# Inverting the diagonal blocks of a delta rule at 32x32 instead of 16x16, with a shorter plan of rounds

## The reference, cut to what matters

```
kb = kc * bc[..., None]
vb = vc * bc[..., None]
Lm = jnp.where(strict, jnp.einsum('nbhid,nbhjd->nbhij', kb, kc) * decay, 0.0)
A = Lm + jnp.eye(C)
rhs = jnp.concatenate([vb, kb * jnp.exp(gc)[..., None]], axis=-1)
sol = triangular_solve(A, rhs, left_side=True, lower=True, unit_diagonal=True)
uc, wc = sol[..., :DV], sol[..., DV:]
...
def step(S, xs):                      # scan over the chunks
    v_new = u_i - w_i @ S
    o = qg_i @ S + qk_i @ v_new
    S = S * gl_i + kg_i.T @ v_new
...
o = rms_norm(o, o_norm_w) * silu(z_b)
```

## Time and profile before

| | before |
|---|---|
| time, median of 3 runs (lowest to highest) | 1189.7 us (1189.56 to 1190.64) |
| the profiled execution's own time | 1193.43 us |
| its span (first to last instruction) | 1191.6 us |
| mean granted TensorE clock of the span | 0.981 |
| TensorE busy | 1154.5 us |
| VectorE busy | 611.9 us |
| ScalarE busy | 359.8 us |
| GpSimd busy | 218.9 us |

### The profile page before, as it was taken

One profiled execution on the slowest core, in us unless ns is written; L12 is line 12 of the kernel. 1 busy time (PEld: TensorE's weight loads), 2 busy tenths in 40 slices (PEclk: granted clock), 3 DMA queues, 4 the chain that ended last, 5 costly groups with the idle time before them and its releaser, 6 DMA issues. The chain is left out here.

```text
span 1191.6 us, 17445 instructions
## 1 busy us (share of the span) xinstructions
PE 1154.5 (97%) x6620; PEld 939.5 (79%) x6620; DVE 611.9 (51%) x1226; ACT 359.8 (30%) x706; POOL 218.9 (18%) x225
## 2 busy tenths in 40 slices
PE   7999999999999999999999999999999999999892
PEld 1588588888878888888788888888788898888671
DVE  2578645555257745563556644552555624445324
ACT  2356322246344211143344211233263301112001
POOL 1244324454200102310000103210000104221000
PEclk9999999999999999999999999999999979999897
DMA  9686754436765732226556621246734512123334
GB/s 369 193 338 226 249 207 158 160 134 223 281 215 209 220 111 90 88 107 239 198 207 211 191 106 72 107 142 230 279 140 146 160 44 100 71 71 107 135 114 166
DMA packets 78998, 203.03 MB, mean 170 GB/s; under 512 B 33674, under 2 KB 43658, under 8 KB 61380
## 3 DMA queue, kind: packets, MB, share of 16 engines
q1 hardware_dynamic: 78916, 201.91, 48.2%
HBM read 151.84 MB, written 50.05 MB: 169 GB/s over the span
## 5 line engine op out<-in xcount | busy, mean ns | idle before, releaser
L1936 PE MATMUL acc<-hhi,wsl 128*128 128x512 f32 x768 | 320.0, 417 | 0.0
L1938 PE MATMUL acc<-hhi,wsl 128*128 128x512 f32 x768 | 301.3, 392 | 0.0
L1937 PE MATMUL acc<-hlo,wsl 128*128 128x512 f32 x768 | 300.4, 391 | 0.0
L1938 PEld LDWEIGHTS acc<-hhi,wsl 128*128 128x128 f32 x768 | 144.6, 188 | 32.2
L1936 PEld LDWEIGHTS acc<-hhi,wsl 128*128 128x128 f32 x768 | 145.0, 189 | 31.4 <-issue 4.5
L1937 PEld LDWEIGHTS acc<-hlo,wsl 128*128 128x128 f32 x768 | 145.3, 189 | 26.5 <-issue 2.2
L1183 DVE SCALAR_TENSOR_TENSOR cacc<-raw,cw,cacc 128x512 f32<-128x512 f32 x144 | 112.8, 783 | 5.1
L1729 POOL TENSOR_TENSOR wsl<-wraw,wsl 128x512 fp32r<-128x512 f32 x64 | 86.2, 1364 | 129.8 <-ACT wsl L882 129.8
L911 ACT ACTIVATE raw<-acc 128x512 f32<-128x512 f32 x48 | 28.7, 597 | 187.3 <-PE acc L1938 179.7
L1180 DVE TENSOR_SCALAR cacc<-raw,cw 128x512 f32<-128x512 f32 x48 | 24.3, 506 | 91.2 <-ACT raw L911 89.7
L919 ACT ACTIVATE tmpa<-acc 128x512 f32<-128x512 f32 x32 | 19.0, 594 | 119.4 <-PE acc L1938 119.4
(11 more groups left out here) (289 smaller groups left out, 1974.4 us busy)
## 6 DMA issues: line engine op xcount, KB each, us to landing
wsl<-kept_w SPq DMA_DIRECT2D x96, 1024.0 KB, 4.8
kept_w<-wsl SPq DMA_DIRECT2D x32, 1024.0 KB, 6.3
wraw<-in_w SPq DMA_DIRECT2D x64, 256.0 KB, 4.2
wada<-in_w_ada SPq DMA_DIRECT2D x8, 1024.0 KB, 13.0
xb<-in_x SPq DMA_DIRECT2D x16, 512.0 KB, 5.5
xres<-in_x SPq DMA_DIRECT2D x16, 512.0 KB, 5.7
out_y<-ytok SPq DMA_DIRECT2D x16, 512.0 KB, 8.2
wada<-in_w_ada SPq DMA_DIRECT2D x16, 256.0 KB, 5.0
```

The costliest lines, as they stand in the source:

```text
L1936: nc.tensor.matmul(acc[t % 2][:], w[:, 0, k], hi[:, k], start=(k == 0), stop=False)
L1937: nc.tensor.matmul(acc[t % 2][:], w[:, 0, k], lo[:, k], start=False, stop=False)
L1938: last = nc.tensor.matmul(acc[t % 2][:], w[:, 1, k], hi[:, k], start=False, stop=(k == KT - 1))
```

## The change

The diagonal blocks that DVE inverts by substitution are 32x32 instead of 16x16. There are 64 of them, on 64 partitions (QB), and the steps are m = 1 to 30 instead of 1 to 14. LEVELS loses its 16. A round has five slots instead of seven, and there are 27 slots instead of 35.

- **Substitution.** It runs in three pieces: m = 1 to 10 after the convolution of tile 8, 11 to 19 after that of tile 9, 20 to 30 after that of tile 10. On DVE `zmul` of tile 12 stands ahead of the third piece, and `zmul` of tile 13 behind it; `zmul` of tile 14 moves to part 23. `inverses` moves from the load turn of tile 10 to that of tile 13, and writes two tiles, `xt` and `xn_`.
- **Plan.** HEAD is 32: four whole tiles (12 to 15) stand ahead of the first slot. FRONT becomes NC*NPREP-1. The last q = 3 falls on p = 6 of the closing slots. The samples' late steps go from slots 30 and 31 to 22 and 23.
- **ScalarE.** The silu of tile 11 moves from ahead of tile 12's tanh to behind that of tile 13.
- **Memory.** `xt` shares space with `ubuf`, `stmp` with `win`; the first u tile of a block waits for `yx`. The gate rows and their weights move to `htmp` and `gpw`, are loaded in block 0 once the samples' activations are turned (a new semaphore), and the row is stored two load turns later; `front_h` of the first block waits for that store.

```diff
-BS = 16
+BS = 32
-LEVELS = (16, 32, 64)
+LEVELS = (32, 64)
+QB = NBK * 16
-SLOTS = (NC + 1) * NPREP
+SLOTS = NC * NPREP + 7
-HEAD = 8
+HEAD = 32
-FRONT = NC * NPREP - 2
+FRONT = NC * NPREP - 1
-SUB_AT = 9
+SUB_AT = {8: (1, 11), 9: (11, 20), 10: (20, BS - 1)}
+INVERSES_AT = 13
...
-    return (r - 1, 3) if r == NC and p == NPREP - 1 else (None, None)
+    return (r - 1, 3) if r == NC and p == 6 else (None, None)
...
-        r, p = divmod(k, NPREP)
+        r, p = divmod(k, NPREP) if k < NC * NPREP else (NC, k - NC * NPREP)
...
-SAMPLE_SLOT = {... "joined": 30, "gate": 30, "pool": 30, "pooled": 31, "mixed": 31}
+SAMPLE_SLOT = {... "joined": 22, "gate": 22, "pool": 22, "pooled": 23, "mixed": 23}
...
+        ru = region("region_u", 4224)
+        ubuf = over("ubuf", ru, 0, [P, 2, BT + PB])
+        xt = over("xt", ru, 0, [QB, BS, BS])
+        rv_ = region("region_v", 4224)
+        win = over("win", rv_, 0, [P, 2, BT + PB])
+        stmp = over("stmp", rv_, 0, [QB, 256])
...
-        grow = ubuf[0:1 + NS].rearrange("p a b -> p (a b)")[:, 0:DM]
-        pwr = win[0:1 + NS].rearrange("p a b -> p (a b)")[:, 0:DM]
+        grow = htmp[0:1 + NS].rearrange("p a b -> p (a b)")
+        pwr = gpw[0:1 + NS]
...
SP, inverses():
-                sp.dma_start(xtd.rearrange("e q x -> q e x"), xtn[:].rearrange("p e j i -> p e (j i)")).then_inc(x_out, 16)
+                for e, blocks in enumerate((xt, xn_)):
+                    sp.dma_start(xtd[e], blocks[:].rearrange("p j i -> p (j i)")).then_inc(x_out, 16)
...
SP, block 0, t == 2:
+                            sp.wait_ge(*h_lo(PROLOGUE, 7))
+                            sp.wait_ge(*done("pe", "hs"))
+                            for dst, src in ((pwr, a["post_w"]), (grow, a["b_gate"])):
+                                sp.dma_start(dst[:], src.to_broadcast([1 + NS, DM])).then_inc(s_prm3, 16)
...
-                        if t == NQ + 6:
+                        if t == NQ + 8:
                             sp.wait_ge(s_trc, 4)
                             sp.dma_start(gate_rows, grow[1:1 + NS]).then_inc(gate_out, 16)
...
-                    if at == SUB_AT + 1:
+                    if at == INVERSES_AT:
                         inverses(it)
...
ACT, block_of():
-                silu_sq(it, NQ - 1)
...
+                        if n == 15:
+                            silu_sq(it, NQ - 1)
...
DVE, block_of():
-                    if t == SUB_AT:
-                        substitute(it)
+                    if t == 10:
+                        zmul(it, NQ)
+                    if t in SUB_AT:
+                        substitute(it, *SUB_AT[t])
+                    if t == 10:
+                        zmul(it, NQ + 1)
...
+                        if n == 23:
+                            zmul(it, t)
...
-                        if n < PARTS and n % 8 == 7 and tile_kind(t)[0] == "z":
+                        if n < PARTS and n % 8 == 7 and tile_kind(t)[0] == "z" and t >= NQ + 3:
                             gated(it, t)
```

More of the change, by code:

```diff
@@ L140, in pool_after @@
     return z - 4 if kind == "z" and z >= 4 else None
-SAMPLE_SLOT = {"spread": 0, "conv": 1, "square": 2, "sums": 4, "root": 5, "delta": 6, "rows": 8, "mean": 8, "joined": 30, "gate": 30, "pool": 30,
-               "pooled": 31, "mixed": 31}
+SAMPLE_SLOT = {"spread": 0, "conv": 1, "square": 2, "sums": 4, "root": 5, "delta": 6, "rows": 8, "mean": 8, "joined": 22, "gate": 22, "pool": 22,
+               "pooled": 23, "mixed": 23}
 SAMPLE_JOBS = ("sp", "sc", "so", "sg", "sb", "s2", "kv", "dt", "son", "spl", "sgt", "sop")
@@ L356, in layer_kernel @@
         raw = sb("raw", [P, RAW, BT + CK - 1])
-        ubuf = sb("ubuf", [P, 2, BT + PB])
-        win = sb("win", [P, 2, BT + PB])
+        ru = region("region_u", 4224)
[4 more added lines that the diff above has]
+        stmp = over("stmp", rv_, 0, [QB, 256])
         rp = region("region_p", 4 * KB)
         pooled = over("pooled", rp, 0, [P, 2, BT])
-        lb = over("lb", rp, 0, [P, BS, BS])
-        xtn = over("xtn", rp, KB, [P, 2, BS, BS])
-        stmp = over("stmp", rp, 3 * KB, [P, 64])
+        lb = over("lb", rp, 0, [QB, BS, BS])
+        xn_ = over("xn_", rp, 0, [QB, BS, BS])
         mt2 = sb("mt2", [P, 2, H, C])
@@ L850, in front_h @@
             act.wait_ge(*job["xf"](it, m))
+            if it == 0 and m == 0:
+                act.wait_ge(gate_out, 16)
             if m >= 2 or it is not PROLOGUE:
@@ L922, in tile @@
                         act.wait_ge(*u_out(it, n - 2))
-                        if it == 0 and n == 0:
-                            act.wait_ge(gate_out, 16)
+                        if n == 0:
+                            act.wait_ge(yx_in, 16 * (it + 1))
                         nc.scalar.activation(ubuf[:, n % 2, PB:], acc[t % 2][:], ACT.Copy).then_inc(u_f.sem, 1)
@@ L1240, in mixing, with substitute @@
                 nc.vector.tensor_tensor(md(c), heads(bank("qk", c)), md(c), ALU.mult).then_inc(mt_f.sem, 1)
[L1242 to L1247, removed]
-                nc.vector.memset(xt.rearrange("p j i -> p (j i)")[:, 0:BS * BS:BS + 1], 1.0).then_inc(sub_f.sem, 1)
-                for m in range(1, BS - 1):
+            def substitute(it, lo, hi):
+                if lo == 1:
+                    dve.wait_ge(lb_in, 16 * (it + 1))
+                    nc.vector.tensor_scalar(xt[:], lb[:], -1.0, None, ALU.mult).then_inc(sub_f.sem, 1)
+                    dve.wait_ge(*sub_f(it, 0))
+                    nc.vector.memset(xt[:].rearrange("p j i -> p (j i)")[:, 0:BS * BS:BS + 1], 1.0).then_inc(sub_f.sem, 1)
+                for m in range(lo, hi):
                     n = BS - 1 - m
@@ L1745, in u_tile @@
                 pool.wait_ge(*u_out(it, g - 2))
-                if it == 0 and g == 0:
-                    pool.wait_ge(gate_out, 16)
+                if g == 0:
+                    pool.wait_ge(yx_in, 16 * (it + 1))
                 held(pool)
```

27 lines of the change are left out of this document (14 added, 13 removed).

## The result

| | before | after |
|---|---|---|
| time, median (lowest to highest) | 1190.2 us (1189.6 to 1191.6, 4 runs) | 1220.5 us (1220.0 to 1220.9, 4 runs) |
| the profiled execution's own time | 1193.4 us | 1220.3 us |
| its span | 1191.6 us | 1218.6 us |
| mean granted TensorE clock | 0.981 | 0.963 |

The changed kernel takes 1.0249 times as long, 95% interval 1.0236 to 1.0261. The forecast was 1200.5 us, with a range to 1212: the sign is right, the size is not. Of the 30.4 us between the medians, 3.3 are no effect of the change: the profiled execution of before lies that much above its median, that of after does not. The spans differ by 27.0 us, and these can be placed.

What follows compares the result with a forecast made beforehand. The prediction took TensorE, busy for 97% of the span, to bound the kernel. Removed matmuls -43.5, junction +8.4, block 0 +7.3, rounds +27.3, clock +11.3 gave +10.8 us on the median 1189.7: 1200.5 us, range 1169 to 1212.

Steps and rivals of the forecast that it cites:

- The step on the rounds: TensorE's turn of ao waits for DVE: nine waits of 1.4 us and three of 4.9, together 27.3 us.
- The step on the substitution: DVE's substitution in three pieces of 7.6, 8.0 and 8.8 us, together 24.4, against 7.0 before.
- the two equations: Price of DVE's substitution from the earlier trace: 0.195 us an operation and 0.00107 us an element.
- The rival of dearer elements: Long broadcast steps on DVE cost double an element: 1240 us, half the effect 1218; chance 0.11, shared with longer slow stretches.
- The junction: Tiles meeting rounds in blocks 1 and 2: tile 15 starts 3.9 us late, 4.2 us a block, 8.4 us in all.
- The gates' transposes: Start of block 0: raw halves of tile 3 some 7 us later on SyncE, the gates' transposes about 1.1 us late.
- The step on the first w: Block 0: SyncE starts the 6.1 us to yx when tile 15 ends, so the first w waits 2.8 us.
- the clock: TensorE's granted clock halves behind three 4.9 us stalls (8.7) and one of 3.9 us (2.6): 11.3 us.
- keep their distance to their users: All other moved steps, such as sample slots, pooling and the gate rows' store, were given no cost.
- the removed work: TensorE loses groups w, xx and yy in 16 chunks, 40.5 us, and late first parts, up to 3: 43.5 us.
- the steady clock: Rival: the stalls come but TensorE's clock stays at its full rate, without the 11.3 us: 1189.2 us; chance 0.17.
- The rounds hide their handovers: Rival: ao reaches TensorE in time, the 27.3 us and their 8.7 of clock go: 1164.5 us; chance 0.22, whole or part.

Runs made afterwards that it cites:

- e1: The changed kernel with the turn of ao for the output projection two slots later (slot 5r+3): 1193.8 us, 1.0023 of the kernel before.
- e5: The changed kernel with FRONT one slot later (NC*NPREP), the turn of ao left in place: 1210.9 us, 1.018 of the kernel before.
- e4: The changed kernel with 16 unused matmuls on TensorE in slot 21 of blocks 0 to 2, where it waits for ao: 1216.9 us.
- e8: e7_all_but_front with FRONT and the samples' delta step one slot later, HEAD 33, and xt written out before its transposed copy: 1169.5 us.
- e10: e8 with block 0's yx read back and next x loaded one load turn later, and the later front only in block 0: 1162.5 us.
- e6_inverses_earlier: The changed kernel with the transfers of the inverses one load turn earlier in SyncE's queue, block 0 only: 1221.0 us, 1.0255 of the kernel before.
- e7_all_but_front: The changed kernel with e1, DVE's work around tiles 8 to 15 recut, the norm's weights loaded two turns later, and e6_inverses_earlier: 1180.7 us.

## Why the prediction was right in its sign and wrong in its size

| term | forecast | measured (spans) |
|---|---|---|
| matmuls removed | -43.5 | -40.8 |
| tiles waiting for zmul, blocks 1 and 2 | +8.4 | +8.4 |
| block 0: tile 15, tile 16, first w, gates' transposes | 2.1 + 1.3 + 2.8 + 1.1 = 7.3 | 2.2 + 0 + 6.1 + 5.3 = 13.6 |
| the turn of ao | +27.3 | +27.6 |
| block 3 | 0 | +3.4 |
| clock | +11.3 | +15.0 |
| sum | +10.8 | +27.2 |

The measured terms are 0.2 us off the 27.0 between the spans; the start of the span has 0.3 of its own (the modulation's weights), and the 0.5 us that the kernel before waited for xv are gone.

**Right.** The step on the rounds: nine waits of 1.4 us were forecast, and they are five of 1.38, one each of 1.41 and 1.47, one of 2.49 (block 0) and one of 0.66 (block 3); and 4.9 for the third of a block, which are 4.54, 4.54 and 5.59. The sum, 27.6 for 27.3, is closer than its parts: 2.49 and 5.59 in block 0 are above, 0.66 and 4.54 below. e1 takes all of them away, e5 the excess of the third ones. The step on the substitution: pieces of 7.6, 8.0 and 8.8 us were forecast, and block 2 has 7.2 (679.60 to 686.8), 7.6 (689.98 to 697.6) and 8.3 (704.09 to 712.4). In the timeline of VectorE, block 2, an operation of 220 elements on 64 partitions:

```profile
704.09 0.37 DVE L1265 TENSOR_TENSOR stmp<-xt,lb 64x220 f32<-64x220 f32 x1
704.50 0.38 DVE L1268 TENSOR_TENSOR xt<-xt,stmp 64x220 f32<-64x220 f32 x1
```

From start to start that is 0.41 us; the two equations on the earlier trace rows give 0.195 + 220 x 0.00107 = 0.43. The rival of dearer elements is out, and that its half price, 1218, is near the 1220.5 is chance. In block 0 seven operations were held up by GpSimd where six were counted, and tile 15 was 2.17 us late for 2.1; the 1.3 us of tile 16 did not come. The junction: 3.15 and 3.16 us ahead of tile 15 for 3.9, and 0.64 and 1.48 ahead of tile 14, where none was forecast. The total, 8.4 for 8.4, is right by luck, by two errors that cancel: the pieces were a little shorter, but lb came later. It has twice the bytes, 256 KB, and landed 4.6 us after its issue (3.0 in the earlier trace rows), so that the zmul of tile 12 was late in its turn.

**Wrong, block 0 (6.3 us of the 16.4).** The gates' transposes were given 1.1 us because the 7 us of SyncE's wait were set against two tiles of cover; the trace has 5.3. The step missed what is queued behind the late raw half on ScalarE: its split waited for the raw half from 53.5 to 62.9 us, the copy of tile 1 stood behind the second half until 66.5, DVE's convolution behind that copy, and the copy of the gates on DVE behind the convolution. The step on the first w named the right chain, and took the time to yx from the earlier trace rows, 6.1 us. The transfers of the changed kernel, median us to landing:

```profile
yx<-inverse_blocks SPq DMA_DIRECT2D x4, 512.0 KB, 5.3
...
inverse_blocks<-xt SPq DMA_DIRECT2D x4, 256.0 KB, 3.0
```

The blocks are twice as wide, so both ways carry twice the bytes; in block 0 the way took 11.1 us, from 177.96 to xv at 189.05. The diff showed the shapes, and the row's 256.0 KB stood beside its 2.1 us: the bytes of a transfer have to be carried over with its time.

**Wrong, the clock (3.7 us).** It was counted behind the 4.9 us waits and one of 3.9. With 0.47 us for each busy one, it cost 6.5 us behind the three turns of ao (13.9 busy) for the 8.7 forecast; but both junctions paid (9.1 busy, 4.2 for 2.6), and so did the late steps of block 0 (71 to 78, 173.5 to 177, 187 to 194: 13.3 busy, 6.2) and one of block 3 (1.6), while the first stretch of block 3 became shorter (17.0 to 10.0 busy, 3.3 less; the samples' rows, 0.3 less). The mechanism is right, as e4 shows; the term was too small because it was counted behind too few of the waits.

**Wrong, block 3 (3.4 us).** The moved steps were said to "keep their distance to their users"; nothing was put for what a step meets on its queue in the new plan. The samples' root and delta steps kept their slots, 5 and 6. Before, GpSimd's power for the samples started at 983.55 us, as soon as DVE's copy ahead of it had ended, at 983.47. In the changed kernel that copy ended at 1034.40, and the power started 4.7 us later, behind the pooling's windows (from 1035.38) and sdec, which now fall into its slot. DVE's steps of slot 6 stand behind the power and ahead of xv (timelines of GpSimd and VectorE of after, block 3):

```profile
1039.08 5.45 POOL L1834 TENSOR_TENSOR rk<-sst,spw 128x32 f32<-128x32 f32 x1
...
1044.56 0.19 DVE L1372 TENSOR_TENSOR dl<-dl,rk 128x32 f32<-128x32 f32 x1 [5.88 <-POOL rk L1834]
```

e8 moves the delta steps to slot 7, with HEAD and FRONT changed as well, and the wait of 1.85 us is gone. The 1.55 us at L2013 have stayed in all kernels here; the step that they wait for (L1364, at 1034.32) stands on DVE behind six others that start from 1031.25 on; whether their order is the cause was not tested.

**Wrong, the removed work (2.7 us).** The groups were priced from the earlier trace rows at 40.5, and up to 3 us were added for a late first part behind each group. The removal measures 40.8, so nearly all of that addition is the error. That its place is this term is argued from the sum, not shown.

**Wrong, the base (3.3 us).** The forecast laid a sum made on one execution on a median 0.3% below it. The profiled execution of the changed kernel took as long as its median. In the kernel before, the time goes with the granted clock of the execution: at 0.985 it took 1189.4 to 1189.8 us, at 0.980 1195.2 to 1195.3, and the profiled one had 0.981. So the base was itself a draw of the clock.

Of the rivals, the steady clock is out by the profile, with eleven stretches at half, and by e4. "The rounds hide their handovers" did not happen, and the price that was put on it (1164.5) is near what e10 measured once they are hidden, 1162.5, though e10 mends more than that rival spoke of.

## What to carry to other kernels

When rounds become shorter, every handover that was laid out in slots becomes shorter with them: list for each consumer in which slot its producer ends, on which queue it stands and behind what, the samples' and the next block's steps too. The matmuls removed were worth 41 us, and a handful of edits of order, with the same work, decided whether the kernel lost 30 or won 28. In a prologue where weights are loaded, split and used through three queues in order, a wait put into the first queue is paid at the last (7.4 us on SyncE came out as 5.3 on TensorE); and a transfer that changes its size needs a price of its own.

## What the runs showed of the hardware

The fall of the clock does not follow from the length of a wait alone. Behind the wait of 2.49 us at 256.9 the changed kernel stayed at full clock, and e6_inverses_earlier, with the same wait at the same place, did not. The stretch from 257 to 260.5 us, first in the changed kernel, then in e6:

```profile
257.00:260.50 3.50, 3.50 (x17) 2.63 (x18) 0.75 (x1) 0.60 (x1) 0.00 (x0) 1.00 0.62 261
```

```profile
257.00:260.50 3.50, 3.23 (x10) 2.76 (x11) 0.96 (x2) 0.00 (x0) 0.00 (x0) 0.51 0.67 281
```

None of the waits of 1.38 us in the changed kernel was followed by it, but one of 1.44 us in e7_all_but_front, at 443.1 us, was:

```profile
444.50:448.00 3.50, 3.50 (x12) 2.75 (x11) 0.45 (x1) 0.12 (x1) 0.00 (x0) 0.52 0.58 241
```

And in e1_ot_later the wait of 3.15 us at 695.7 was followed by half clock (696.6 to 700.0), while behind that of 3.12 at 442.1, the same step of the block before, the clock stayed at 1.00. A forecast can give such a wait only a chance.

In block 0 an operation of the substitution took 1.20, 1.36 and 1.34 us where the same shapes take 0.36 to 0.38 in block 2; GpSimd was at the weights' split then (timelines of VectorE and GpSimd of the changed kernel):

```profile
147.37 3.00 POOL L1808 TENSOR_TENSOR sk<-sk,half 128x16 f32<-128x16 f32 x1
148.04 0.40 DVE L1268 TENSOR_TENSOR xt<-xt,stmp 64x238 f32<-64x238 f32 x1
...
160.27 1.20 DVE L1265 TENSOR_TENSOR stmp<-xt,lb 64x220 f32<-64x220 f32 x1
...
162.90 0.37 DVE L1265 TENSOR_TENSOR stmp<-xt,lb 64x210 f32<-64x210 f32 x1
...
158.69 3.94 POOL L1748 TENSOR_TENSOR wsl<-wraw,wsl 128x512 fp32r<-128x512 f32 x3 [8.00 <-ACT wsl L893]
```

All seven operations of the substitution in block 0 that start during an instruction of the split end 0.1 to 0.3 us after it; these instructions take 1.3 to 1.45 us each. But beside GpSimd's power for the norms (147.37, 3.00 us) the operations took 0.40 us as elsewhere, so it is not any work on GpSimd that holds them up. The Trainium skill, "SBUF — State Buffer", section "Who interferes with whom", says that DVE and GpSimd share a pair of ports under an exclusive lock, and that a DVE instruction with two inputs in SBUF contends with a GpSimd instruction that reads SBUF; the trace agrees for the split, and shows no such delay beside the power.
